# A two-layer diffusion step on one core: the attention items' scores issued two ahead, and three smaller moves

## What is computed

```python
for l in range(DEPTH):                                   # DEPTH = 2
    sh1, sc1, gt1, sh2, sc2, gt2 = _modulation(silu(c), w_ada[l], b_ada[l])
    h = _rmsnorm(x, norm_mix_pre[l]) * (1.0 + sc1) + sh1
    y = mixer(h)       # w_in, then four head groups A, B, C, D, then w_o
    x = x + gt1 * _rmsnorm(y, norm_mix_post[l])
    h = _rmsnorm(x, norm_ffn_pre[l]) * (1.0 + sc2) + sh2
    x = x + gt2 * _rmsnorm(_channel_mixer(h), norm_ffn_post[l])
```

## Time and profile before

| | us |
|---|---|
| median of 3 runs (lowest, highest) | 1674.35 (1673.54, 1676.71) |
| profiled execution, its own time | 1674.89 |
| its span, first to last instruction | 1673.1 |
| PE busy in the span | 1576.5 (94%) |
| DVE busy | 1194.3 (71%) |
| ACT busy | 976.9 (58%) |
| mean granted clock of TensorE | 0.966 |

### The profile page before, as it was taken

The page is one execution under the profiler, slowest core; times in us unless marked ns, Lnnn a source line. Parts: engine busy times, 40 slices in busy tenths (PEclk is TensorE's granted clock), DMA queues, the critical chain, the costliest instruction groups (busy, mean ns, idle before and its releaser), DMA issues.

```text
span 1673.1 us, 22863 instructions
## 1 busy us (share of the span) xinstructions
PE 1576.5 (94%) x8167; PEld 1295.3 (77%) x8167; DVE 1194.3 (71%) x1014; ACT 976.9 (58%) x958; POOL 89.1 (5%) x142
## 2 busy tenths in 40 slices
PE   5998899999989868999999999999999999999996
PEld 2866789988777747888888888888888888888885
DVE  2556444534556425888888888888888888888885
ACT  4343444434534344776776776776776776776773
POOL 2410040000020010000000000000000000000001
PEclk8999899999989778999999999999999999999998
DMA  9864484577634344998998998998998998998991
GB/s 370 274 195 150 165 257 153 186 240 280 236 117 152 126 152 146 367 368 321 360 371 321 359 369 320 362 365 323 363 363 321 363 365 321 364 365 320 365 366 50
DMA packets 218291, 473.87 MB, mean 283 GB/s; under 512 B 8464, under 2 KB 41536, under 8 KB 218240
## 3 DMA queue, kind: packets, MB, share of 16 engines
q1 hardware_dynamic: 215024, 466.38, 78.3%
q0 software_dynamic: 3216, 6.79, 1.6%
HBM read 470.62 MB, written 2.52 MB: 283 GB/s over the span
## 4 chain that ended last, share of the span: by engine, by line
PE 89%; DVE 4%; ACT 2%; DMA 2%; issue 1%; POOL 1%; POOLq 0%; SPq 0%; DVEq 0%; ACTq 0%
PE ps L1541 22%; PE ps L1546 22%; PE ps L1542 22%; PE ps L1556 3%; PE ps L1557 3%; PE ps L1563 3%; PE ps L1922 2%; PE ps L1751 2%; DMA raw<-in_w_ada 2%; PE ps L1934 1%; PE ps L1715 1%; PE ps L1586 1%; PE ps L1625 1%; DVE w_lo L1060 1%; PE ps L1597 1%
## 5 line engine op out<-in xcount | busy, mean ns | idle before, releaser
L1060 DVE TENSOR_TENSOR w_lo<-raw,w_hi 128x2048 fp32r<-128x2048 f32 (+1 forms) x397 | 903.4, 2284 | 204.7 <-ACT w_hi L712 203.6
L712 ACT ACTIVATE w_hi<-raw 128x2048 fp32r<-128x2048 f32 (+1 forms) x397 | 757.5, 1913 | 254.0 <-PE ps L1542 237.1
L1541 PE MATMUL ps<-w_hi,x_hi 128*128 128x512 f32 (+1 forms) x1216 | 435.2, 370 | 6.5 <-ACT w_hi L712 2.7
L1542 PE MATMUL ps<-w_hi,x_lo 128*128 128x512 f32 (+1 forms) x1216 | 426.7, 363 | 0.0
L1546 PE MATMUL ps<-w_lo,x_hi 128*128 128x512 f32 (+1 forms) x1216 | 284.4, 364 | 0.0
L1541 PEld LDWEIGHTS ps<-w_hi,x_hi 128*128 128x128 f32 x1216 | 228.8, 188 | 47.1 <-issue 7.8
L1542 PEld LDWEIGHTS ps<-w_hi,x_lo 128*128 128x128 f32 x1216 | 228.8, 188 | 36.1
L1546 PEld LDWEIGHTS ps<-w_lo,x_hi 128*128 128x128 f32 x1216 | 206.6, 188 | 39.6
L1541 PE MATMUL ps<-w_hi,h_hi 128*128 128x512 f32 x528 | 207.8, 394 | 0.0
L1542 PE MATMUL ps<-w_hi,h_lo 128*128 128x512 f32 x528 | 207.4, 393 | 0.0
L1546 PE MATMUL ps<-w_lo,h_hi 128*128 128x512 f32 x528 | 141.2, 392 | 0.0
(11 more groups left out here) (242 smaller groups left out, 1213.1 us busy)
## 6 DMA issues: line engine op xcount, KB each, us to landing
raw<-in_moe_w_gate SPq DMA_DIRECT2D x112, 1024.0 KB, 5.2
raw<-in_moe_w_up SPq DMA_DIRECT2D x112, 1024.0 KB, 5.3
raw<-in_moe_w_down SPq DMA_DIRECT2D x112, 1024.0 KB, 5.2
raw<-in_w_ada SPq DMA_DIRECT2D x48, 1024.0 KB, 5.4
raw<-in_w_in SPq DMA_DIRECT2D x20, 960.0 KB, 11.6
raw<-in_ffn_w_gate SPq DMA_DIRECT2D x11, 1024.0 KB, 5.4
raw<-in_ffn_w_up SPq DMA_DIRECT2D x11, 1024.0 KB, 6.4
raw<-in_ffn_w_down SPq DMA_DIRECT2D x11, 1024.0 KB, 5.2
```

Source lines behind the costliest of these rows:

```text
L712: act.activation(split_hi(c, slice(0, width(c))), raw[:, r % NRAW, 0:width(c)], ACT.Copy).then_inc(hi_done, 1)
L1060: dve.tensor_sub(split_lo(c, n), raw[:, raw_of(c) % NRAW, n], split_hi(c, n)).then_inc(lo_done, 1)
L1541: pe.matmul(out, xh, split_hi(c, w), start=start, stop=False, skip_group_check=True)
L1542: last = pe.matmul(out, xl, split_hi(c, w), start=False, stop=False, skip_group_check=True)
```

## The change

It has these parts.

- PE issues the scores two items ahead: both first scores before the loop, then for item i the transposes first and the scores of i + 2 after them. `exps` on ACT and `soft_pre` on DVE are two ahead too, and `soft_T(i)` now stands before `soft_pre(i + 2)`. Each stream has two probability buffers, `probs_all`, which lie over `x_hi` and `x_lo`.
- `LATER` becomes C2, C5, C3, C4. The scores of group C wait for all but the last of these steps, and `item_out` of C waits for the last.
- Map pieces 20 and 21 are multiplied with items 8 and 9, so `out_projection` has only 22 and 23 left, one ahead of `norm_T` and one behind it. `STREAM` has 20 and 21 ahead of the last two units of `w_o`. `o_T` moves to banks 0, 1 and 4, 5, and `out_T` no longer waits for the evacuation of section 4.
- Splits of `w_o` units stand behind items 6 to 9: one, none, one, one. The third was behind the first `x_hi` before.
- `rows(l, 3)` and `rows(l, 4)` on ACT stand at the end of items 3 and 7.
- POOL loads the router once the last item of layer 1 has been evacuated (`o_evac` 20).
- In layer 1 ACT evacuates section 5 and splits the second expert unit before it squares stream 1's rows (`norm_sq`), where it did so after.

```diff
--- before.py
+++ after.py
@@ -68,7 +68,7 @@
 FIRST = [["A", "B0", "B1", "D", "K", "C1"], ["A", "B0", "B1", "D", "Dc", "K", "BM", "C1"]]
-LATER = ["C2", "C3", "C4", "C5"]
+LATER = ["C2", "C5", "C3", "C4"]
@@ -122,12 +122,12 @@
             units += win[:2] + ada(1, 8, 9, 10, 11) + win[2:]
-        units += ada(l, 12, 13, 14, 15, 16, 17) + wo[:1] + ada(l, 18) + wo[1:2] + ada(l, 19) + wo[2:]
+        units += ada(l, 12, 13, 14, 15, 16, 17) + wo[:1] + ada(l, 18) + wo[1:2] + ada(l, 19, 20, 21) + wo[2:]
         if l == 0:
-            units += ffn[:2] + ada(0, 20, 21, 22, 23) + ffn[2:23] + ada(1, 4, 5) + ffn[23:26] + ada(1, 6, 7) + ffn[26:29]
+            units += ffn[:2] + ada(0, 22, 23) + ffn[2:23] + ada(1, 4, 5) + ffn[23:26] + ada(1, 6, 7) + ffn[26:29]
...
         else:
-            units += ada(1, 20, 21, 22, 23)
+            units += ada(1, 22, 23)
@@ -241,7 +241,7 @@
         x_hi = sb("x_hi", [P, 2, D], F32R)
-        probs = nc.alloc_sbuf_tensor_at("probs", [P, 2, 4, 256], F32, offset=x_hi_at)
+        probs_all = nc.alloc_sbuf_tensor_at("probs", [P, 2, 2, 4, 256], F32, offset=x_hi_at)
@@ -412,7 +412,7 @@
-            return ps[:, 6:8, :] if s == 0 else ps[:, 4:6, :]
+            return ps[:, 4 * s:4 * s + 2, :]
@@ -430,6 +430,10 @@
             return ps[:, 4:6, :].rearrange("p a (b k) -> p (a b) k", b=2)
+
+        def probs(i):
+
+            return probs_all[:, i // 2 % 2, i % 2, :, :]
@@ -680,6 +684,9 @@
                     rstd(stat[:, o + 8:o + 12], stat[:, o:o + 4], HD * EPS, drs)
+                if l:
+                    pool.wait_ge(o_evac, 20)
+                    pool.dma_start(rtr, router[0].rearrange("(k p) e -> p k e", p=P)).then_inc(in_rtr, 16)
@@ -691,8 +698,6 @@
                         norm_rstd(1, 0, s)
-            pool.wait_ge(x_upd, 6)
-            pool.dma_start(rtr, router[0].rearrange("(k p) e -> p k e", p=P)).then_inc(in_rtr, 16)
@@ -788,8 +793,8 @@
                 for h in range(4):
-                    src = probs[:, s, h, 0:nk] if biased else score_view(s)[:, h, :]
-                    last = act.activation(probs[:, s, h, 0:nk], src, ACT.Exp, bias=sm[:, s, 4 + h:5 + h],
+                    src = probs(i)[:, h, 0:nk] if biased else score_view(s)[:, h, :]
+                    last = act.activation(probs(i)[:, h, 0:nk], src, ACT.Exp, bias=sm[:, s, 4 + h:5 + h],
@@ -988,19 +993,20 @@
                     rows(0, 2)
+                for i in range(2):
+                    exps(l, i)
                 for i in range(10):
-                    if i in (4, 8):
-                        rows(l, 2 + i // 4)
-                    exps(l, i)
...
                         prep(l, len(FIRST[0]) + i // 2)
-                    if i in (6, 8):
-                        split_to(wo_u(l, 0) + i // 2 - 2)
+                    if i + 2 < 10:
+                        exps(l, i + 2)
+                    if i in (3, 7):
+                        rows(l, 3 + i // 4)
+                    if i >= 6:
+                        split_to(wo_u(l, 0) + {6: 1, 7: 1, 8: 2, 9: 3}[i])
...
                     act.activation(x_hi[:, s, :].rearrange("p (a b) -> p a b", a=2), o_T(s), ACT.Copy).then_inc(o_hi, 1)
-                    if s == 0:
-                        split_to(wo_u(l, 0) + 3)
@@ -1017,9 +1023,10 @@
                     norm_hi(l, 1, 0)
+                else:
+                    rows(l, 5)
+                    split_to(wo_u(l, 2) + 2)
                 norm_sq(l, 1, 1)
-                if l:
-                    rows(l, 5)
@@ -1179,7 +1186,7 @@
                 if it == "D" and s == 1:
-                    pv = probs[:, 1, :, :]
+                    pv = probs(i)
@@ -1473,10 +1480,11 @@
                 soft_pre(l, 0)
+                soft_pre(l, 1)
                 for i in range(10):
-                    if i + 1 < 10:
-                        soft_pre(l, i + 1)
                     soft_T(l, i)
+                    if i + 2 < 10:
+                        soft_pre(l, i + 2)
@@ -1708,7 +1714,7 @@
                 if i >= 8:
-                    pe.wait_ge(prep_evac[s], np_(s) * (l + 1))
+                    pe.wait_ge(prep_evac[s], np_(s) * (l + 1) - 1)
@@ -1727,12 +1733,14 @@
                     for h in range(4):
-                        last = pe.transpose(ps[:, kb, cols(h, P)], probs[:, i % 2, h, cols(kb, P)], ident())
+                        last = pe.transpose(ps[:, kb, cols(h, P)], probs(i)[:, h, cols(kb, P)], ident())
...
                 n = 10 * l + i
+                if it == "C":
+                    pe.wait_ge(prep_evac[s], np_(s) * (l + 1))
@@ -1773,13 +1781,14 @@
                 item_scores(l, 0)
+                item_scores(l, 1)
                 for i in range(10):
-                    if i + 1 < 10:
-                        item_scores(l, i + 1)
                     item_T(l, i)
+                    if i + 2 < 10:
+                        item_scores(l, i + 2)
...
                         prep(l, i % 2, len(FIRST[i % 2]) + i // 2)
-                        ada(l, 12 + i)
+                    ada(l, 12 + i)
@@ -1788,7 +1797,6 @@
                 pe.wait_ge(o_evac, 10 * l + 9 + s)
-                pe.wait_ge(row_evac, SECTIONS.index((l, 4)) + 1)
@@ -1812,10 +1820,9 @@
                                 gates(l, 0, s, n, n)
-                ada(l, 20)
+                ada(l, 22)
                 norm_T(l, 1, 0)
-                for n in (21, 22, 23):
-                    ada(l, n)
+                ada(l, 23)
...
                 def gate_up(t, c, up):
```

## The result

The changed kernel takes 1649.62 us, the median of four executions (1647.8 to 1654.2). The kernel before, timed beside it, takes 1673.94 us, also four (1673.44 to 1676.71). The ratio is 0.9856, 95% interval 0.9832 to 0.9879: 24.3 us, or 1.4%, faster. The forecast was 1651.0, range 1645 to 1661. The profiled execution took 1654.2 us, its span is 1652.4, so 1.8 lies around it as before; it is the slowest of the four.

The account below looks back on a forecast made before the run. PE was taken as the bound, 89% of the chain, with gains only where it idles or runs at half clock. Attention 6.4, norm -1.0 and router 18.0 sum to 23.4 off 1674.35: 1651.0 us, range 1645 to 1661.

Parts of the forecast that it names:

- The router, 18.0: Projection to DVE's router part: 18.0 us sooner, 9.6 from the load's wait, the rest from slow matmuls and the second unit's split.
- the walk: The new order followed on three engines with trace durations, giving attention's waits and the router part's start; sum 23.4 us.
- The 16.3 us from there to the first expert product stay: From DVE's router part to the first expert product: the stretch keeps its 16.3 us.
- the experts pass it on whole: Experts: the router's gain goes through undiminished, as ACT there waits for PE, 237 of 239 us, not for transfers.
- Attention, 6.4: Second half of attention, items 6 to 9: 3.2 us less in each layer, 6.4 together, by scores two ahead.
- clock term: Second half of each attention: 0.9 us added for half clock, beside 22.2 of work and 7.2 of waits.
- clean case: Rival: full clock in both attentions (8.2), 18.6 at the router, norm loses nothing, gather at full clock; 1645.9 us, chance 0.2.
- The norm, 1.0 lost: Layer 0's norm: without pieces 20 and 21 the gap may slow the next products; bounds 0 and 2.9, 1.0 us lost.
- nothing is won: Layer 0's norm: taking pieces 20 and 21 out lengthens the x_lo wait from 1.22 to 3.1 us, so no gain.
- Only the wait goes: Rival at the router: another chain fills the rest, only 9.6 us gained; 15.0 off in all, 1659.4 us, chance 0.1.
- Half clock stays: Rival: -0.5 in each attention, 17.0 at the router, -2.9 in the norm; 13.1 off, 1661.3 us, chance 0.18.
- The split waiting for its transfer: Slower rival: ACT's moved split waits for its transfer, holding up stream 1's norm; 1679 us if landing at 630, chance 0.02.

Follow-up runs that it names:

- second profiled execution: The changed kernel timed and profiled once more, with nothing altered: median 1649.8 us of five, ratio 0.9846 to the kernel before.
- attention alone: Changed kernel with router load, ACT order behind it and map pieces 20 and 21 put back as before: 1667.3 us, ratio 0.9963 to the kernel before.
- late load: Changed kernel with only the router's load put back behind the norm (x_upd 6): 1663.77 us, ratio 0.9938 to the kernel before.
- late split: Changed kernel with section 5's rows after the squares and the second expert unit's split after stream 1's modulation: 1656.01 us, ratio 0.9886.
- map pieces back: Changed kernel with only map pieces 20 and 21 put back behind the output projection: 1653.94 us, ratio 0.9881 to the kernel before.
- products in seven waits: Changed kernel with moved DVE splits plus unused PE products in seven waits; map pieces in attention, both back, or one back: 1635.94, 1634.67, 1631.5 us.
- load alone: Kernel before with only the router's load moved to the last item's evacuation: 1660.14 us, ratio 0.9924.
- DVE order: Changed kernel with the second w_o split behind soft_T(9) and the third behind the first x_lo on DVE: 1644.75 us, ratio 0.9828.
- four products before the gather: Changed kernel with four unused 128x512 products in PE's wait before the first gather: 1648.3 us, ratio 0.9846.

## Why the prediction was right, and where it was not

**The router, 18.0.** Measured 17.9 to DVE's router part, and the reasons hold: undoing the load costs 14.0 and doing it alone gives 13.6, more than its wait of 9.59; the order on ACT costs 6.2 when it is undone. The walk had gates at full clock; they took 3.66 us, at half, as did `columns` (1.71) and stream 1's transposes (1.94) ahead of them, and the logits behind them 1.85, at full: that is between the walk's 18.6 and 17.0. The taking of 18.0 between these two was a choice, so that it came out to 0.1 is in part luck. The late-next chain was as told (DVE's split of the third unit, waiting 3.50 us for ACT). The load's 7.2 us were hidden; put back, it took 6.2 and the wait was 12.05, so the case of a load of 2 us and a wait of 7 falls.

**"The 16.3 us from there to the first expert product stay", "the experts pass it on whole".** True in the second profiled execution (16.23 and 1023.41), false in the first (17.79 and 1024.83). The wait before the gather, 4.43 us, and the one of 2.42 behind it each put the work that follows at half clock in some executions. Up to 2.9 us are lost so that the sum has nowhere.

**Attention, 6.4.** In the profiled execution the two attentions gave 3.75 and 5.62, together 9.4, so the term was too small by a third. That attention alone also gives 6.4 is a coincidence: by the walk that kernel, without the map pieces, should give 8.4. (The two layers' 3.24 and 3.35 add up to 6.6, too, and not to 6.4.) The three waits of the walk came where it put them, shorter in sum: 1.65, 2.15 and 3.4 us forecast, 1.04, 2.16 and 2.42 measured in layer 0, and 1.03, 2.15 and 3.08 in layer 1. The clock term was off in both layers. I had it as 0.9; layer 0 paid about 2.4, its busy time of 24.18 us less layer 1's 21.76 (clock 0.87, `item_out(9)` at 3.65 us), and layer 1 nothing (1.00, 1.97 us). So layer 0 came near its forecast, 29.79 for 30.3, by errors that cancel, and layer 1 took 28.03 us where the clean case had 22.2 + 7.2, 29.4.

**The norm, 1.0 lost.** The wait before the dense mixer is 2.94 us (forecast 3.1) and the first unit takes 4.44 us from its first product to `norm_T`, where it took 2.91: 1.5 lost, and with the 0.31 of the stretch ahead of it 1.8. The row that ends this unit before the change, to be read with the earlier trace rows:

```profile
214.58 1.03 PE L1611 MATMUL ps<-cst,xn 128*128 128x128 f32 x8
```

Here the row after 1.22 us of waiting misled: a wait of 2.94 did bring half clock. All fourteen profiled executions bear this out: the unit takes 2.8 to 2.9 us in all five with a wait of 1.22 and in all three with one of 0.16 to 0.17, and 4.4 to 5.3 in five of the six with one of 2.93 or 2.94. The Trainium skill (TensorE: Matmul & The Clock Gate, "HAM oscillation — how this bites in real kernels") had it that way round, and this trace agrees in direction, with half of the 2.9 us that I priced by it; the case it tells of is a kernel that waits for a transfer before every group. It is no sure rule: in the sixth, with the late load, whose code up to there is that of the changed kernel but for the load on POOL, the same wait (2.9 us by the groups of instructions below) has full clock behind it, and the stretch from there to layer 1's attention takes 290.15 us and not 294.74.

```profile
L1561 PE MATMUL ps<-w_hi,x_hi 128*128 128x256 f32 x14 | 3.4, 288 | 2.9 <-DVE x_lo L1130 2.9
```

The mean of a product of 128x256 is 288 ns there; in the changed kernel, in the same window, it is 418.

**The dense mixer, at nothing.** No edit touches it, and it took 3.56 us more (3.38 in the second profile). Most of what is beyond the first unit is one place, a wait of 2.67 us for ACT's `w_hi` that is in both kernels. PE there, before and after:

```profile
372.70 0.36 PE L1541 MATMUL ps<-w_hi,x_hi 128*128 128x256 f32 x1 [2.67 <-ACT w_hi L712]
...
376.55 2.05 PE L1546 MATMUL ps<-w_lo,x_hi 128*128 128x256 f32 x16
```

```profile
370.80 0.36 PE L1547 MATMUL ps<-w_hi,x_hi 128*128 128x256 f32 x1 [2.67 <-ACT w_hi L717]
...
374.88 0.41 PE L1548 MATMUL ps<-w_hi,x_lo 128*128 128x256 f32 x1
...
376.18 2.05 PE L1552 MATMUL ps<-w_lo,x_hi 128*128 128x256 f32 x16
```

From the wait's end to the products with `w_lo` it takes 3.85 us before and 5.38 after, with the same instructions: in the latter, products that take 0.28 us at the unit's start take 0.41 in its middle, as at 374.88. With 1.53 in the first unit and 1.53 here, 3.1 of the 3.56 are found. Why the clock falls there in one kernel and not in the other stays open; it fell in the profiled executions of the changed kernel (both), of the late split, of the map pieces back, of attention alone and of the three kernels with products in seven waits, and not in those of the late load, the load alone, the DVE order (with the map pieces in either place) and the four products before the gather. The late load and the four products have the code of the changed kernel up to there, on PE, ACT and DVE.

**The map pieces, "nothing is won".** This step failed, though the total hid it. It looked at the wait in layer 0's norm alone. In layer 1 section 5's rows stand before the squares on ACT, piece 23 comes ahead of them, and so the pieces' place decides whether PE waits 0.66 or 2.87 us, with logits at half clock behind the latter. By the medians this place is worth 4.1 and 5.0 us in two pairs of kernels without products. I had priced what the moved pieces cover, but not who waits for their result.

**The rivals.** "Only the wait goes" fell by both load experiments. "Half clock stays" didn't come true as a whole: layer 1's attention and stream 1's logits were at full clock, the gates, the gather and the mixer's first unit at half. "Clean" came in layer 1's attention. The split waiting for its transfer isn't seen: ACT starts it at 595.40 without waiting for it. Against the walk's 23.4 the profiled execution has 3.0 more in attention, 0.1 less at the router, 2.9 less in norm and mixer, 2.9 less behind the router, and 0.2 at the start: 20.7, the difference of the spans. It is the slowest of its four executions, and between the medians it is 24.3. So the 1.4 us between 1651.0 and 1649.62 flatter the sum: attention, norm with mixer, and all behind the router were each off by 3 us, and in part these errors cancel.

## What to carry to other kernels

When a step is moved off an engine's stretch, follow its result too: the map pieces were worth 4 to 5 us by the medians, and what they cost when they were put back shows not at the waits that they had filled, but behind the queue on ACT that begins with their rows. After shortening waits look at what stands behind the short ones that are left: a wait of 2 to 3 us before a dense group can cost 1.5 to 2.4 us more in clock, and useless products in seven such waits gave 9 us here, a queue order that removes one in each layer 3 to 5. And when a stretch that no edit touches changes, as the dense mixer did, profile again before a cause is looked for, and look at other kernels with the same code there: the second profile of the changed kernel repeated it (3.38 us for 3.56), and only that of the late load, with 4.6 us less, showed it to be no fixed cost.

## What was not expected of the hardware

- PE doing more, uselessly, makes the kernel shorter: with products in seven waits 1635.94 against 1644.75 us, mean clock 0.987 against 0.977 in the profiled executions.
- The same wait has full clock behind it in one execution and half in another: 2.42 us before the first expert unit (0.39 or 0.63 us a product), 2.67 us in the dense mixer. Even ahead of attention, where no kernel here differs from another on PE, the stretch to item 0's transposes takes 108.45 to 111.51 us. That this makes all of the spread between executions is not shown, since one of each kernel or two were profiled; the nine of the changed kernel spread over 8.0 us (1646.21 to 1654.2).
- The clock can be at half without a long wait: stream 0's transposes in the router part run at half clock (1.91 us, 1.07 at full) behind nothing but a wait of 0.94 and logits of 8 columns, in the changed kernel; in that with the DVE order the same row takes 1.07.
- A load of 32 KB took 7.1 us from issue to landing beside the weight stream in the kernel before, and 6.2 with the late load.
